# Opening of a two-layer trunk: modulation blocks that hold shifts and scales of the same 256 features, and a first double in pairs of contraction tiles

## The chip, the core and the metric

The kernel runs on one core of one Trainium2 chip. The metric is the device time of one execution in microseconds; the median of the runs counts. The core's engines run side by side and meet at semaphores: TensorE (PE, matrix products; its weight loads are PEld), VectorE (DVE), ScalarE (ACT), GpSimd (POOL) and SyncE (SP), which here issues DMAs.

## What is computed

Two trunk layers run over 128 context tokens and 512 denoising tokens, 1024 features wide. Each sub-layer is normed and modulated by vectors that come from a conditioning vector: c_ctx for the context tokens, c for the others. What matters here is the first sub-layer:

```
mod = (silu(c) @ w_mod[l] + b_mod[l]).reshape(1, 1, 3 * N_SUB, D_MODEL)
def modulated(j, y):
    return _rmsnorm(y, g[j]) * (1 + mod[:, :, 3 * j + 1]) + mod[:, :, 3 * j]
def _swiglu(h, w_in, w_out):
    g, u = jnp.split(h @ w_in, 2, axis=-1)
    return (jax.nn.silu(g) * u) @ w_out
x = x + 0.5 * mod[:, :, 2] * _swiglu(modulated(0, x), ffn_w_in[l, 0], ffn_w_out[l, 0])
```

So the first product of the network needs a shift (columns 0 to 1023 of w_mod[0]) and a scale (columns 1024 to 2047) for each of the 1024 features, each a sum over 1024 rows of w_mod.

## The kernel before

Tokens stand in the free dimension, features on the partitions: x is 8 tiles (kt = 0 to 7) of 128 features by 640 tokens. The tokens are handled in two halves of 320 (hf 0 and 1). A product in full precision is three matmuls (split_product): high part by high part, low by high and high by low, where the weights' parts are w_hi (ScalarE) and w_lo (VectorE) and the activations' parts b_hi and b_lo.

The two feed-forward products of a sub-layer are done in doubles of two output tiles of gate and of up. A double behind the first has seven items of 24 matmuls, which need sums and differences of the activations' quadrants (z11, z12, z21, z22; t1 and t2 are such sums; b_hi and b_lo hold seven forms of them). The first double of a sub-layer is plain: for a half hf, a tile k, a group g (gate or up) and a column block s there is one part (plain_part) of three matmuls: 64 parts, 192 matmuls. A part waits for the low part of its form and, at its group's first tile, for its w_lo (item_lo; one w_lo serves four tiles of one group).

Modulation for the first norm: the 2048 columns of w_mod are loaded as four blocks of 512 columns (mod_first), 2 MB each: 0 and 1 are shifts, 2 and 3 scales, and block 0 with block 2 serves tiles 0 to 3, block 1 with 3 tiles 4 to 7 (FIRST_ORDER). SyncE issues, in this order, the identity, x, seven small rows (b_mod, c_ctx, c, gains), block 0, block 2, the weights of the first two items, block 1, the weights of the other two, block 3. PE turns x into features (L1945), then the small rows (L1949), sums a block by 16 matmul instructions of 512 columns on four 32-row groups (mod_rows_of, L1970); ScalarE copies the sums out (keep_rows, L2583), PE multiplies them by pick, which turns them into columns on the partitions (turn_first, L1977), and VectorE adds the bias and multiplies (keep_first with keep_mod, L2698 and L2701). The inverse of the norm is spread over the partitions by PE (spread_first, L1959) and kept by ScalarE (L2068) in ss.

A tile then runs: VectorE scales x by ss (scale_form, L2754, two tiles at once), VectorE shifts the context tokens (L2763), ScalarE scales and shifts the rest (L2075) and makes b_hi (L2145, L2147, L2143), VectorE makes b_lo (L2829, L2824). The order on PE is written out in opening_double, on ScalarE and VectorE in opening_norm. Behind the forms VectorE makes t1 and t2 (L2848, L2850), products for the gate (L2846), sums of weights (L2664) and the w_lo of the second double (L2643). SyncE loads later blocks of w_mod (mod_grain, last_grain) once rows_free lets it; they are summed by features in instructions of 256 columns (mod_products, L1251) and turned by VectorE in squares of 32 (L2711).

## Time and profile before

| what | us |
|---|---|
| median of 3 runs | 2340.64 |
| the runs | 2340.48 to 2345.56 |
| profiled execution | 2343.96 |
| its span | 2342.2 |
| PE busy in the span | 2318.6 |
| first product of the first double | 29.27 |

The page gives busy time by engine, the chain of work that ended last, and groups of instructions by line. The chain is followed back from the end: each step goes to what released it. In the opening the timeline and the waits tell which engine is late; behind it the chain is almost one row of matmuls of line L1104. Matmul ends are modelled, so starts are what is read. A window gives the busy time of each engine in a stretch, the granted share of TensorE's clock and the DMA rate.

### The profile page before, as it was taken

Reading aid. Unit: us, or ns where it says so; the run is one execution under the profiler, and the core shown is the slowest. Engines: PE = TensorE matmul, PEld = TensorE weight load, DVE = VectorE, ACT = ScalarE, POOL = GpSimd, SP = SyncE. Lnnn points to the kernel's source line nnn. Section 1 sums busy time; section 2 is a strip of 40 time slices with the busy share of each in tenths; the row PEclk is TensorE's granted clock in tenths of the full one; section 3 lists DMA queues with packets and bytes.
Section 4 is the critical chain, followed back from the end, with each engine's and each line's share of the span. In section 5 each row is a group of like instructions: output and inputs, shape, how many; then the busy total and the mean of one; then the engine's idle time right before and its main releaser. Section 6 shows DMA issues by size and latency. Waiting matters only on the chain.

```text
span 2342.2 us, 39079 instructions
## 1 busy us (share of the span) xinstructions
PE 2318.6 (99%) x16276; PEld 2234.1 (95%) x16276; DVE 1567.4 (67%) x2376; ACT 955.7 (41%) x1501; POOL 30.5 (1%) x44
## 2 busy tenths in 40 slices
PE   7999999999999999999999999999999999999999
PEld 6999999988789999999999999999999999999999
DVE  4886776657867876777587777676245768467473
ACT  6532423443655523414364243244215355244242
POOL 0000000000001000000010000000000010000000
PEclk9999999999999999999999999999999999999999
DMA  8342554421101253334224344225221012322122
GB/s 299 126 145 90 198 162 139 150 89 54 57 19 55 91 162 127 122 112 148 88 92 160 114 156 148 87 77 173 87 75 46 19 55 73 108 73 91 57 97 73
DMA packets 199017, 251.56 MB, mean 107 GB/s; under 512 B 13026, under 2 KB 172602, under 8 KB 198842
## 3 DMA queue, kind: packets, MB, share of 16 engines
q1 hardware_dynamic: 198698, 249.00, 32.2%
q8 instruction: 129, 2.11, 0.4%
q14 instruction: 46, 0.38, 0.1%
q10 hardware_dynamic: 144, 0.07, 0.0%
HBM read 245.76 MB, written 3.28 MB: 106 GB/s over the span
## 4 chain that ended last, share of the span: by engine, by line
PE 94%; DVE 3%; ACT 2%; DMA 1%; issue 1%; SPq 0%; POOL 0%; DVEq 0%; ACTq 0%
PE banks L1104 82%; PE banks L1251 1%; PE banks L1428 1%; PE banks L1430 1%; PE banks L1429 1%; PE banks L1587 1%; DMA w_raw<-ffn_w_in 1%; PE banks L1575 1%; PE banks L1602 1%; PE banks L1796 0%; ACT w_hi L2032 0%; PE banks L1260 0%; PE banks L1970 0%; PE banks L1298 0%; DVE w_lo L2643 0%
## 5 line engine op out<-in xcount | busy, mean ns | idle before, releaser
L1104 PE MATMUL banks<-b_hi,w_hi 128*128 128x320 f32 x2496 | 776.9, 311 | 6.2 <-DVE b_lo L2829 3.5
L1104 PE MATMUL banks<-b_lo,w_hi 128*128 128x320 f32 x2496 | 772.2, 309 | 0.0
L1104 PE MATMUL banks<-b_hi,w_lo 128*128 128x320 f32 x2496 | 772.2, 309 | 0.0
L1104 PEld LDWEIGHTS banks<-b_hi,w_hi 128*128 128x128 f32 x2496 | 469.5, 188 | 20.2 <-issue 13.0
L2032 ACT ACTIVATE w_hi<-w_raw 128x1024 fp32r<-128x1024 f32 x296 | 310.2, 1056 | 401.9 <-PE banks L1104 226.1
L1104 PEld LDWEIGHTS banks<-b_lo,w_hi 128*128 128x128 f32 x2496 | 469.7, 188 | 0.0
L1104 PEld LDWEIGHTS banks<-b_hi,w_lo 128*128 128x128 f32 x2496 | 469.5, 188 | 0.0
L2643 DVE TENSOR_TENSOR w_lo<-w_raw,w_hi 128x1024 fp32r<-128x1024 f32 x296 | 361.5, 1223 | 150.2 <-ACT w_hi L2032 148.7
L1104 PE MATMUL banks<-hid_hi,w_hi 128*128 128x320 f32 x1664 | 400.2, 311 | 0.5 <-DVE hid_lo L2938 0.5
L1104 PE MATMUL banks<-hid_hi,w_lo 128*128 128x320 f32 x1664 | 396.2, 309 | 0.0
L1104 PE MATMUL banks<-hid_lo,w_hi 128*128 128x320 f32 x1664 | 396.1, 309 | 0.0
L1104 PEld LDWEIGHTS banks<-hid_hi,w_hi 128*128 128x128 f32 x1664 | 282.4, 188 | 2.1 <-issue 0.9
L1104 PEld LDWEIGHTS banks<-hid_lo,w_hi 128*128 128x128 f32 x1664 | 282.9, 188 | 0.0
L1104 PEld LDWEIGHTS banks<-hid_hi,w_lo 128*128 128x128 f32 x1664 | 282.4, 188 | 0.0
L2671 DVE SCALAR_TENSOR_TENSOR x<-banks,mod,x 128x128 f32<-128x128 f32 x354 | 135.1, 434 | 218.0 <-PE banks L1104 218.0
L2664 DVE TENSOR_TENSOR w_raw<-w_raw 128x1024 f32<-128x1024 f32 x160 | 195.4, 1222 | 17.6 <-DMA w_raw<-ffn_w_in 11.7
L2038 ACT ACTIVATE w_hi<-w_raw 128x1024 fp32r<-128x1024 f32 (+1 forms) x96 | 93.2, 984 | 233.4 <-PE banks L1104 233.2
L2217 ACT ACTIVATE hid_hi<-work 128x640 fp32r<-128x640 f32 x88 | 64.3, 735 | 155.3 <-DVE work L3023 142.0
L2649 DVE TENSOR_TENSOR w_lo<-w_raw,w_hi 128x1024 fp32r<-128x1024 f32 (+1 forms) x96 | 107.6, 1132 | 9.4 <-ACT w_hi L2038 8.7
L2990 DVE TENSOR_TENSOR work<-work,banks 128x320 f32<-128x320 f32 x80 | 38.1, 485 | 79.9 <-ACT work L2246 79.9
L2626 DVE TENSOR_TENSOR w_lo<-w_raw,w_hi 128x2048 fp32r<-128x2048 f32 (+1 forms) x24 | 52.8, 2201 | 54.7 <-ACT w_hi L2021 54.7
L2021 ACT ACTIVATE w_hi<-w_raw 128x2048 fp32r<-128x2048 f32 (+1 forms) x26 | 48.0, 1847 | 98.1 <-PE banks L1104 48.7
(339 smaller groups left out, 2409.1 us busy)
## 6 DMA issues: line engine op xcount, KB each, us to landing
w_raw<-ffn_w_in SPq DMA_DIRECT2D x176, 512.0 KB, 4.8
mod_grain<-w_mod SPq DMA_DIRECT2D x78, 512.0 KB, 5.9
w_raw<-ffn_w_out SPq DMA_DIRECT2D x64, 512.0 KB, 4.5
last_grain<-w_mod SPq DMA_DIRECT2D x40, 512.0 KB, 5.6
w_raw<-ffn_w_out SPq DMA_DIRECT2D x32, 384.0 KB, 3.7
w_raw<-w_in_odd SPq DMA_DIRECT2D x20, 512.0 KB, 4.7
mod_first<-w_mod SPq DMA_DIRECT2D x3, 2048.0 KB, 15.2
w_raw<-w_in_even SPq DMA_DIRECT2D x12, 512.0 KB, 4.9
```

What stands on the lines that cost most here:

```text
L1104: ins = pe.matmul(o, w3[w], v3[v][cols], start=first and i == 0, stop=last and i == 2, skip_group_check=onto_read)
L1251: ins = pe.matmul(bank[MODB][b * MOD_ROWS:(b + 1) * MOD_ROWS, 0:KIND_COLS], wide_c[:, kt, :], by_features(grain[q])[:, b], start=kt == 0, ...
L2021: act.activation(split_view(w_hi, kind, parity(unit)), raw_view(kind, parity(unit)), ACT.Copy).then_inc(hi_ready, 1)
L2032: act.activation(ring_in(w_hi, in_slot(d, t)), operand(d, t), ACT.Copy).then_inc(hi_ready, 1)
L2038: act.activation(ring_out(w_hi, out_slot(c, u), CHUNKS[c]), out_operand(c, u), ACT.Copy).then_inc(hi_ready, 1)
L2217: act.activation(hid_hi[:, k + s, :], work[:, s, 0:2, :].rearrange("p a b -> p (a b)"), ACT.Copy)\
L2626: dve.tensor_tensor(split_view(w_lo, kind, parity(unit)), raw_view(kind, parity(unit)), split_view(w_hi, kind, parity(unit)).bitcast(F32), ...
L2643: dve.tensor_tensor(ring_in(w_lo, q), operand(d, t), ring_in(w_hi, q).bitcast(F32), ALU.subtract).then_inc(lo_ready, 1)
L2649: dve.tensor_tensor(ring_out(w_lo, q, n), out_operand(c, u), ring_out(w_hi, q, n).bitcast(F32), ALU.subtract)\
L2664: dve.tensor_tensor(out_, in0, in1, op).then_inc(sums_done, 1)
L2671: ins = dve.scalar_tensor_tensor(out=xs, in0=bank[banks[hf]][:, in_bank], scalar=mod_col(v, layer, 3 * j + 2, d), in1=xs, op0=ALU.mult, op ...
L2990: dve.tensor_tensor(work[:, s, 1, :], work[:, s, 1, :], role(d, s, "C"), ALU.add).then_inc(c12_done, 1)
```

## The change

A block now holds 256 features' shifts and the same features' scales: block n serves the tiles 2n and 2n+1. It is loaded by two DMAs of 256 columns per row each (pieces of 1 KB in place of 2 KB); block 3 goes by four DMAs into the grain buffers and first_tail, after the sums of block 0. The order on SyncE is block 0, weights, block 1, block 2, weights, block 3. The seven small rows are issued by ScalarE.

The sums are taken by features: for each of 8 row tiles four instructions of 128 columns (64 on the engine, first_sums_of), and VectorE turns them in squares of 32 (first_turn). The copy by ScalarE, the turn by PE and pick are gone. SiLU comes ahead of the squares; of the ten copies of turned x ScalarE takes two (X_BY_ACT) and VectorE eight, before five and five.

The first double runs by pairs n of tiles: the four parts of half 0 for each tile of the pair, then the sums of block n+1, then three of four parts of half 1 (SUM_LESS leaves out group 1, block 1); the last part of each tile follows behind the last pair. The norm's work on ScalarE and VectorE follows in the same pairs, and the first sum of forms t1 stands behind pair 1.

```diff
         mod_first = [place(f"mod_first{r}", [P, KT, MOD_COLS], at=at) for r, at in
-                     enumerate((HB + TT * D * 4, HD_AT + 24576, HB + TT * D * 4 + block_bytes, HB + 71680 - block_bytes))]
+                     enumerate((HB + TT * D * 4, HD_AT + 24576, HB + 71680 - block_bytes))]
+        first_tail = place("first_tail", [P, 2, MOD_COLS], at=HB + TT * D * 4)
...
-        mod_rows = place("mod_rows", [P, 2, MOD_COLS], at=WORK + 5120)
+        first_turn = place("first_turn", [P, MOD_TILES, MOD_ROWS], at=WORK + 5120)
...
-        FIRST_BANK = (3, 2, 1, 7)
-        FIRST_SUM_BANK = (0, 1, 7, 7)
+        FIRST_SUM_BANK = (5, 1, 1, 1)
+        X_BY_ACT = (0, 2)
+        HEAD_LEAD = GRAIN_BUFS - 1
+        SUM_LESS = ((0, 0), (0, 1), (1, 0))
...
+        def first_rows(n, kt):
+
+            if n < QUAD - 1:
+                return mod_first[n][:, kt, :]
+            if kt < 2 * HEAD_LEAD:
+                return mod_grain[:, kt // 2, kt % 2 * MOD_COLS:(kt % 2 + 1) * MOD_COLS]
+            return first_tail[:, kt - 2 * HEAD_LEAD, :]
...
-            def load_first(r):
-                for hf in range(2) if r == 2 else (None,):
-                    ks = slice(0, KT) if hf is None else slice(HK * hf, HK * (hf + 1))
-                    sp.dma_start(mod_first[r][:, ks, :], w_mod[0][:, ks, r * MOD_COLS:(r + 1) * MOD_COLS])\
-                        .then_inc(mod_second_half_in if hf == 1 else mod_first_in[r], 16)
+            def load_first(n):
+
+                if n == QUAD - 1:
+                    sp.wait_ge(mod_first_sum, 1)
+                for j in range(2):
+                    c0 = j * D + n * (MOD_COLS // 2)
+                    src, cols = w_mod[0][:, :, c0:c0 + MOD_COLS // 2], slice(j * MOD_COLS // 2, (j + 1) * MOD_COLS // 2)
+                    if n < QUAD - 1:
+                        sp.dma_start(mod_first[n][:, :, cols], src).then_inc(mod_first_in[n], 16)
+                    else:
+                        lead = mod_grain[:, :, :].rearrange("p i (k c) -> p (i k) c", c=MOD_COLS)
+                        sp.dma_start(lead[:, :, cols], src[:, 0:2 * HEAD_LEAD, :]).then_inc(mod_first_in[n], 16)
+                        sp.dma_start(first_tail[:, :, cols], src[:, 2 * HEAD_LEAD:KT, :]).then_inc(mod_first_in[n], 16)
             load_first(0)
-            load_first(2)
             load_in(0, 0, 0)
             load_first(1)
+            load_first(2)
             load_in(0, 0, 1)
             load_first(3)
...
-            def opening_double(late_mod):
-
-                plain_parts(0, 0, range(2), range(2))
-                late_mod(0)
-                plain_parts(0, 0, range(2, HK), range(2))
-                late_mod(1)
-                plain_parts(0, 1, range(2), (0,))
-                late_mod(2)
-                plain_parts(0, 1, range(2, HK), (0,))
+            def opening_double(next_sums):
+
+                for n in range(QUAD):
+                    ks = range(2 * n, 2 * n + 2)
+                    plain_parts(0, 0, ks, range(2))
+                    if n == 0:
+                        pe.wait_ge(inverse_kept_in[1], 1)
+                    if n + 1 < QUAD:
+                        next_sums(n + 1)
+                        for k in ks:
+                            for g, s in SUM_LESS:
+                                plain_part(0, 1, k, g, s)
                 pe.wait_ge(first_kept, QUAD)
-                plain_parts(0, 1, range(HK), (1,))
-                plain_parts(0, 0, range(HK, KT), range(2))
-                plain_parts(0, 1, range(HK, KT), (0,))
-                plain_parts(0, 1, range(HK, KT), (1,))
+                for k in range(HK):
+                    plain_part(0, 1, k, 1, 1)
...
-            def mod_rows_of(r, into):
-
-                pe.wait_ge(mod_first_in[r], 16)
+            def first_sums_of(n):
+
+                sums = bank[FIRST_SUM_BANK[n]][:, 0:MOD_TILES * MOD_ROWS]
+                pe.wait_ge(mod_first_in[n], 16 * 2 if n < QUAD - 1 else 16 * 4)
+                if n > 0:
+                    pe.wait_ge(first_kept, n)
                 for kt in range(KT):
-                    if r == 2 and kt == HK:
-                        pe.wait_ge(mod_second_half_in, 16)
-                    group = slice(kt % 4 * MOD_ROWS, (kt % 4 + 1) * MOD_ROWS)
-                    ins = pe.matmul(into[group, :], wide_c[:, kt, :], mod_first[r][:, kt, :], start=kt < 4, stop=kt >= 4)
+                    cols = first_rows(n, kt).rearrange("p (m b c) -> p b m c", b=QUAD, c=MOD_ROWS)
+                    for b in range(QUAD):
+                        ins = pe.matmul(sums[b * MOD_ROWS:(b + 1) * MOD_ROWS, :], wide_c[:, kt, :], cols[:, b],
+                                        start=kt == 0, stop=kt == KT - 1)
                 ins.then_inc(mod_first_sum, 1)
 
-            def turn_first(n):
-
-                pe.wait_ge(mod_rows_ready, n + 1)
-                for m in range(MOD_TILES):
-                    ins = pe.matmul(bank[FIRST_BANK[n]][:, 2 * m:2 * m + 2], mod_rows[:, n % 2, m * P:(m + 1) * P], pick[:, :],
-                                    start=True, stop=True)
-                ins.then_inc(first_turned, 1)
-
+            spread_first(0)
             pe.wait_ge(silu_ready, 1)
-            pe.wait_ge(pick_ready, 1)
-            pe.wait_ge(x_kept_act, TT)
-            pe.wait_ge(x_kept_dve, TT)
-            mod_rows_of(0, bank[FIRST_SUM_BANK[0]])
-            for hf in range(2):
-                spread_first(hf)
-            turn_first(0)
-            mod_rows_of(2, bank[FIRST_SUM_BANK[1]])
-            turn_first(1)
-
-            def late_mod(step):
-
-                if step == 0:
-                    pe.wait_ge(inverse_kept_in[1], 1)
-                    mod_rows_of(1, bank[FIRST_SUM_BANK[2]])
-                elif step == 1:
-                    turn_first(2)
-                    mod_rows_of(3, bank[FIRST_SUM_BANK[3]])
-                else:
-                    turn_first(3)
-            ffn(0, late_mod, None, 1)
+            first_sums_of(0)
+            spread_first(1)
+            pe.wait_ge(x_kept_act, len(X_BY_ACT))
+            pe.wait_ge(x_kept_dve, 2 * TT - len(X_BY_ACT))
+            ffn(0, first_sums_of, None, 1)
...
-                    act.wait_ge(first_kept, 2 if kt < HK else QUAD)
+                    act.wait_ge(first_kept, kt // 2 + 1)
...
-            def opening_norm(keep_rows):
-
-                for kt in range(HK):
-                    if kt < 2:
-                        item_hi(0, 0, kt)
-                    form_high(0, 0, kt, 0)
-                for kt in range(HK):
-                    form_high(0, 0, kt, 1)
-                    if kt == 1:
-                        keep_rows(2)
-                item_hi(0, 0, 2)
-                item_hi(0, 0, 3)
-                keep_rows(3)
-                for hf in range(2):
-                    for kt in range(HK, KT):
-                        form_high(0, 0, kt, hf)
+            def opening_norm():
+
+                for n in range(QUAD):
+                    for hf in range(2):
+                        for kt in (2 * n, 2 * n + 1):
+                            if n == 0 and hf == 0:
+                                item_hi(0, 0, kt)
+                            form_high(0, 0, kt, hf)
+                    if n == 1:
+                        item_hi(0, 0, 2)
+                        item_hi(0, 0, 3)
                 sum_forms(0)
...
+            b_rows = a["b_mod"].rearrange("l (r p) -> l r p", p=P)
+            for l in range(DEPTH):
+                act.dma_start(small_rows[0:3 * N_SUB * KT, l, :], b_rows[l]).then_inc(rows_in, 16)
+            act.dma_start(small_rows[0:KT, 2, :], a["c_ctx"].rearrange("(r p) -> r p", p=P)).then_inc(rows_in, 16)
+            act.dma_start(small_rows[KT:2 * KT, 2, :], a["c"].rearrange("b (r p) -> (b r) p", p=P)).then_inc(rows_in, 16)
+            act.dma_start(small_rows[2 * KT:8 * KT, 2, :], a["norm_gain"].rearrange("l s (r p) -> (l s r) p", p=P))\
+                .then_inc(rows_in, 16)
+            act.dma_start(small_rows[64:68, 2, :], a["sgu_gain"].rearrange("e g p -> (e g) p")).then_inc(rows_in, 16)
+            act.dma_start(small_rows[68:72, 2, :], a["identity"][0:4, :]).then_inc(rows_in, 16)
+            act.wait_ge(rows_kept, 1)
+            given = rows_t[:, 0:2 * KT].rearrange("p (v k) -> p v k", v=2)
+            act.wait_ge(wide_cleared, 1)
+            act.activation(wide_c[:, :, 0:2].rearrange("p k v -> p v k"), given, ACT.Silu).then_inc(silu_ready, 1)
+            sqrt_table()
...
+                def scale_pair(n):
+                    for hf in range(2):
+                        scale_form(0, 0, slice(2 * n, 2 * n + 2), hf)
+
+                scale_form(0, 0, slice(0, 2), 0)
+                for n in range(QUAD):
+                    keep_first(n)
+                    for kt in (2 * n, 2 * n + 1):
+                        shift_first(kt)
+                        if n == 0:
+                            item_lo(0, 0, kt)
+                            if kt == 0:
+                                scale_form(0, 0, slice(0, 2), 1)
+                        low_form(0, slice(kt, kt + 1), 0)
+                    if n + 1 < QUAD:
+                        scale_pair(n + 1)
+                    low_form(0, slice(2 * n, 2 * n + 2), 1)
+                    if n == 1:
+                        first_form_sum(0)
+                        item_lo(0, 0, 2)
+                        item_lo(0, 0, 3)
...
             def keep_first(n):
 
-                r = FIRST_ORDER[n]
-                dve.wait_ge(first_turned, n + 1)
-                sums = bank[FIRST_BANK[n]][:, 0:2 * MOD_TILES].rearrange("p (m v) -> p v m", v=2)
-                keep_mod([sums[:, v, :] for v in range(2)], slice(MOD_TILES * r, MOD_TILES * (r + 1)))
+                def pair(tile):
+                    return tile[:, 0:2 * KT].rearrange("p (j k) -> p j k", j=2)[:, :, 2 * n:2 * n + 2]
+                dve.wait_ge(mod_first_sum, n + 1)
+                chain.inc(dve.transpose(first_turn[:, :, :].rearrange("p m c -> p (m c)"),
+                                        bank[FIRST_SUM_BANK[n]][:, 0:MOD_TILES * MOD_ROWS]))
+                chain.wait()
+                for v in range(2):
+                    chain.inc(dve.tensor_tensor(mod_tmp[:, v, :].rearrange("p (j k) -> p j k", j=2),
+                                                first_turn[:, :, v].rearrange("p (j k) -> p j k", j=2), pair(mod_add), ALU.add))
+                chain.wait()
+                for v in range(2):
+                    chain.inc(dve.tensor_tensor(pair(mod[:, v, :]), mod_tmp[:, v, :].rearrange("p (j k) -> p j k", j=2),
+                                                pair(mod_mul), ALU.mult))
+                chain.wait()
                 dve.sem_inc(first_kept, 1)
```

Two places in the order of the built programs. On PE, from the end of the turns of x to the second half's first products: before, two blocks' sums and two turns stand ahead of the first product.

```order
L1949 MATMUL banks_5<-ident,small_rows 128x72 x3
L1970 MATMUL banks_1<-mod_first_93,wide_c 32x512 x8
L1959 MATMUL banks_7<-ident,x_rms 128x128 x2
L1959 MATMUL banks_7<-ident,x_rms 128x64 x2
L1959 MATMUL banks_7<-ident,x_rms 128x128 x2
L1977 MATMUL banks_3<-pick,mod_rows 128x2 x4
L1970 MATMUL banks_1<-mod_first_95,wide_c 32x512 x8
L1977 MATMUL banks_3<-pick,mod_rows 128x2 x4
L1104 MATMUL banks_3<-b_hi,w_hi 128x320
L1104 MATMUL banks_3<-b_lo,w_hi 128x320
L1104 MATMUL banks_3<-b_hi,w_lo 128x320
```

After (order of the changed kernel): one block's sums stand there, between the two spreads.

```order
L1961 MATMUL banks_1<-ident,x_rows 128x128 x8
L1971 MATMUL banks_7<-ident,x_rms 128x128 x2
L1971 MATMUL banks_7<-ident,x_rms 128x64
L1984 MATMUL banks_5<-mod_first_92,wide_c 32x128 x32
L1971 MATMUL banks_7<-ident,x_rms 128x64
L1971 MATMUL banks_7<-ident,x_rms 128x128 x2
L1108 MATMUL banks_3<-b_hi,w_hi 128x320
L1108 MATMUL banks_3<-b_lo,w_hi 128x320
L1108 MATMUL banks_3<-b_hi,w_lo 128x320
```

What moved: the small rows' turn to the front, the second block's sums behind 24 products, and the steps with pick away.

On VectorE, from the last work on tile 3 to the first low part of tile 4: before, one w_lo, then columns, scalings, another w_lo, columns.

```order
L2824 TENSOR_TENSOR b_lo<-z_81,b_hi 128x640 x2
L2643 TENSOR_TENSOR w_lo<-w_raw,w_hi 128x1024
L2698 TENSOR_TENSOR mod_tmp<-banks_1,mod_add 128x4 x2
L2701 TENSOR_TENSOR mod<-mod_tmp,mod_mul 128x4 x2
L2754 TENSOR_TENSOR z_83<-x,ss 128x640 x2
L2643 TENSOR_TENSOR w_lo<-w_raw,w_hi 128x1024
L2698 TENSOR_TENSOR mod_tmp<-banks_7,mod_add 128x4 x2
L2701 TENSOR_TENSOR mod<-mod_tmp,mod_mul 128x4 x2
L2763 TENSOR_SCALAR z_a<-z_a,mod 128x128 x4
L2829 TENSOR_TENSOR b_lo<-z_a,b_hi 128x320 x2
```

After, between the low part of the wide half of tiles 2 and 3 and the first low part of tile 4:

```order
L2802 TENSOR_TENSOR b_lo<-z_80,b_hi 128x640
L2818 TENSOR_TENSOR t_83<-z_80,z_a 128x1280
L2632 TENSOR_TENSOR w_lo<-w_raw,w_hi 128x1024 x2
L3587 STREAM_TRANSPOSE first_turn<-banks_1 128x128
L3591 TENSOR_TENSOR mod_tmp<-first_turn,mod_add 128x4 x2
L3595 TENSOR_TENSOR mod<-mod_tmp,mod_mul 128x2x2 x2
L2741 TENSOR_SCALAR z_a<-z_a,mod 128x128
L2807 TENSOR_TENSOR b_lo<-z_a,b_hi 128x320
```

What moved: t_83 (before it was t_84, behind all forms) and both w_lo stand in a row ahead of the columns of block 2.

## Rows read from the trace of the kernel before

**Rows 1.** The page: busy time of TensorE, and the chain that ended last.
```profile
PE 2318.6 (99%) x16276; PEld 2234.1 (95%) x16276; DVE 1567.4 (67%) x2376; ACT 955.7 (41%) x1501; POOL 30.5 (1%) x44
...
PE 94%; DVE 3%; ACT 2%; DMA 1%; issue 1%; SPq 0%; POOL 0%; DVEq 0%; ACTq 0%
```

**Rows 2.** The chain in order of time, 60 to 120 us: start, us, what.
```profile
59.86 23.61 PE banks L1104 x161
83.48 1.86 PE banks L1251 x32
```

**Rows 3.** The same chain, 0 to 60 us.
```profile
11.02 1.14 ACT squares L2571 x2
...
16.80 2.87 PE banks L1970 x16
...
29.27 6.21 PE banks L1104 x24
35.47 1.85 PE banks L1970 x16
37.32 3.71 PE banks L1104 x24
41.04 0.79 PE banks L1977 x8
...
43.68 1.95 PE banks L1104 x12
...
46.42 13.59 PE banks L1104 x92
```

**Rows 4.** Waits of PE, 0 to 120 us: in total, times, longest.
```profile
PE banks L1104 <- DVE b_lo L2829: 3.0, 1, 3.0
```

**Rows 5.** DMA issues up to 60 us: count, KB each, us to landing.
```profile
x_rows<-x_prompt SPq DMA_DIRECT2D x1, 512.0 KB, 3.9
...
ident<-identity SPq DMA_DIRECT2D x1, 64.0 KB, 2.0
```

**Rows 6.** Windows: stretch, length, busy us (instructions) per engine, PEclk, DMA share, GB/s.
```profile
0.00:9.60 9.60, 3.87 (x17) 3.50 (x18) 1.65 (x9) 3.70 (x6) 0.20 (x4) 1.00 0.79 290
...
17.70:21.00 3.30, 3.30 (x19) 1.61 (x11) 0.19 (x1) 1.24 (x3) 0.00 (x0) 0.50 1.05 383
21.50:23.50 2.00, 2.00 (x23) 1.39 (x25) 0.54 (x5) 0.55 (x2) 0.00 (x0) 1.00 1.10 348
...
28.00:34.60 6.60, 5.33 (x20) 5.37 (x21) 6.56 (x13) 5.68 (x11) 0.00 (x0) 0.50 1.07 369
```

**Rows 7.** Timeline, VectorE and ScalarE, 24 to 29 us: start, duration, operation.
```profile
24.90 0.82 DVE L2754 TENSOR_TENSOR z<-x,ss 128x640 f32<-128x640 f32 x1
26.33 0.23 DVE L2698 TENSOR_TENSOR mod_tmp<-banks,mod_add 128x4 f32<-128x4 f32 x2 [0.61 <-PE banks L1977]
...
27.24 1.22 DVE L2643 TENSOR_TENSOR w_lo<-w_raw,w_hi 128x1024 fp32r<-128x1024 f32 x1
...
28.63 0.48 DVE L2829 TENSOR_TENSOR b_lo<-z_a,b_hi 128x320 fp32r<-128x320 f32 x1
...
25.08 1.05 ACT L2032 ACTIVATE w_hi<-w_raw 128x1024 fp32r<-128x1024 f32 x1
26.92 0.55 ACT L2075 ACTIVATE z_a<-z_a,mod 128x192 f32<-128x192 f32 x1 [0.79 <-DVEq L3609]
27.50 0.47 ACT L2145 ACTIVATE b_hi<-z_a 128x320 fp32r<-128x320 f32 x1
```

**Rows 8.** The tile mod_turn: min/median/max ns of the transposition.
```profile
L2711 DVE STREAM_TRANSPOSE mod_turn<-banks x32: 307/314/318, 128.6 to 1642.1; 128x128 f32<-128x128 f32 x32
```

**Rows 9.** Timeline of VectorE, 55 to 76 us.
```profile
55.23 0.83 DVE L2829 TENSOR_TENSOR b_lo<-z,b_hi 128x640 fp32r<-128x640 f32 x1 [1.28 <-ACT b_hi L2143]
55.97 1.48 DVE L2848 TENSOR_TENSOR t<-z,z_a 128x1280 f32<-128x1280 f32 x1
...
74.58 1.22 DVE L2643 TENSOR_TENSOR w_lo<-w_raw,w_hi 128x1024 fp32r<-128x1024 f32 x1
```

125 lines of the change are left out of this document (36 added, 89 removed).

## The prediction

> **What bounds the kernel now.** I read the page's busy shares and its chain first [rows 1]: TensorE (PE) is busy 99% of a span of 2342.2 us and carries 94% of the chain that ended last. So a microsecond counts only if it moves the row of matmuls on PE. The chain behind the opening is that row alone: 161 products in 23.61 us, 0.1466 us each, then modulation sums, then products again [rows 2]. Nothing there depends on the clock on the wall, so what the opening gains at its last wait is kept to the end; what it gains before that can be lost again. The chain of the opening [rows 3] shows where PE starts its first product: 29.27, after a wait of 3.0 us for the first low part [rows 4]. From there PE never waits before 120 us (the other waits of that list lie ahead of 29.27). The first double has 192 products; before, they end at 46.42 + 132 x 0.1466 = 65.8.
>
> **The start.** Everything here is re-laid, so I walk the new order with the old durations. SyncE no longer issues the seven small rows; ScalarE does, at 0.3 to 0.4 us each, the last at about 3. No row shows such a DMA land in the shadow of the x rows. The identity alone took 2.0 us, the x_prompt rows 3.9 [rows 5]; I take 4.0 for each, the side of the one that shared the stream, so the last is in at 6.9. PE turns them first, VectorE copies, SiLU ends at 8.6, a table load of 1.3 at 9.9, two x copies at 0.5 and five squares at 1.14 [rows 3] end at 17.1, the root, its reciprocal and PE's spread of the first half at 18.2.
> In sentences that the rest can do without: the Trainium skill, page "DMA: Bandwidth & Descriptors", section "Issuing engines are not separate DMA queues", says that DMAs of different issuing engines share the same 16 DMA engines and interleave, so that a second issuer saves issue time alone. No row of before has two issuers at once. By it the rows still compete with x, which speaks against the early end of my bounds, not for a later start than the rival below.
> Block 0 lands in time: 2.8 MB were through by 9.6 at 290 GB/s [rows 6], and the blocks, now in pieces of 1 KB, should go at the 348 GB/s of the stretch of 1 KB weights (21.5 to 23.5) and not at the 383 of the blocks of before (17.7 to 21.0) [rows 6]. That is 2.1 MB, 15.6, plus about 1 us until the semaphore, 16.8; the first weights (1 MB) then land at 19.8. Block 3 lands near 41, far ahead of its use at 49, so the slower pieces cost nothing; w_raw too is covered.
> Sums of block 0: now 64 instructions of 128 columns instead of 16 of 512. Before, 16 of 512 took 1.85 [rows 3] and 32 of 256 took 1.86 [rows 2]: the same columns, the same time, whatever the cut. I take 1.86 for 64 of 128 too. The other end is that an instruction doesn't get shorter than the 0.058 of the 256-column ones: 3.7 per block.
> So: 18.2 + 1.9 = 20.1, spread of the second half 20.7, ScalarE keeps it 21.2, w_hi 1.05, w_lo 1.22, one scaling 0.82 (pitch 0.75), b_lo 0.48 [rows 7]. The column work (transposition 0.31 [rows 8], two additions and two products 0.23 a pair [rows 7]) lies beside the ScalarE steps. PE starts at **24.6**, 4.65 earlier than 29.27.
>
> **The rest of the first double.** I take the first 24 products as before, 6.2, most of them at half clock: granted 0.50 in 28.0 to 34.6, the lower of the two levels of 1.2 and 2.4 GHz, after PE had stood idle before 29.27 [rows 6]. A run of products behind other work costs 0.19 more than its count (24 in 3.71, 12 in 1.95 [rows 3]). The new order on PE: 24 products to 30.8; sums of block 1, 32.7; 18 products, 35.5; 24 products, 39.0; sums of block 2, 40.9; 18 products, 43.7. Now the pair 4, 5 must be ready, and it isn't. VectorE has done the pair 2, 3 at 36.7, then stand two scalings (1.5), a low part of 0.82 that waits for ScalarE until 38.4, the first sum of forms (1.48) and two w_lo (2.3): it is free at 42.8, 1.6 after the sums came. Then transposition, columns, shift, b_hi and b_lo (0.9 + 0.55 + 0.47 + 0.48, with handing over): 45.3. **A new stall of 1.6 us.** Go on: 24 products to 48.8; sums of block 3, 50.7; 18 products, 53.5 (they cover the same chain of 2.6 for the last pair); 66 products, 63.2. Against 65.8 that is 2.6 earlier. The sum of it: start +4.65, two turn steps of 0.79 gone behind the start [rows 3], one more block's sums on the path -1.86, one switch more -0.2, stall -1.6.
>
> **The work behind it, where VectorE was nearly late already.** In before VectorE runs without a gap from its last wide b_lo at 55.23 to the w_lo at 74.58, which ends at 75.80 [rows 9]. PE reads that weight in item 3 of the second double, which starts two items of 24 products ahead of 83.48 [rows 2]: 76.44. The slack was 0.6. After: sums of block 3 seen by VectorE at 51.1, columns 52.0, four shifts with their b_hi on ScalarE (0.95 to 1.05 each with handing over, [rows 7]) and one wait for a shift to 56.5, b_lo at 56.6. From 55.23 to 75.80 are 20.57; the first sum of forms (1.48, pitch 1.52 [rows 9]) was done earlier, which leaves 19.05: 75.65. PE arrives at 63.2 + 3 x 3.52 = 73.8. **PE waits 1.9 us**, and item 3 starts at 75.7 instead of 76.44. Of 4.65 us at the start 0.7 are left. Behind that the order on all engines is the old one.
>
> **The sum.** The profiled execution takes 2343.96 (span 2342.2), the median of the runs is 2340.64, 3.3 below, with runs to 2345.56; the saving is taken off the median: 2340.64 - 0.7 = 2339.9. A difference under 0.3% (7 us) is about what a measurement of this kernel can't tell from no change.
>
> **The rivals.**
> 1. The wait at item 3 isn't there, because VectorE or ScalarE runs its stretch some tenths quicker at each handing over, or the rows land early (2.0 each, the low bound, is 0.8 more). For it: the wait is the difference of two long walks. Against: VectorE had no idle time there to give. Then all 2.6 are kept: 2338.0, and with the higher clock a few products sooner 2337.
> 2. The half clock or late rows take the start: slower than before. PE stands idle from about 14 to 17.6, as it did ahead of 16.80, where the clock went to 0.50 in 17.7 to 21.0 [rows 6] and the sums took 2.87 instead of 1.85 [rows 3]. With sums and spreads of block 0 wholly at half clock the start moves by up to 2.5, with rows landing only behind all of x (9.6) by 3.4. It decides from a start 0.7 later than 24.6, since from there on all goes through ScalarE's and VectorE's chain to item 3. Part of the delay comes back when the higher clock comes at an earlier product; net 0.9 to 2.2 slower than before: 2341.5 to 2342.8. For it: the same idle time, the same place. Against: the spread and the sums begin sooner after the last turn.
> 3. Sums by 128 columns cost as much an instruction as those of 256. Then 1.86 more in each of four blocks, 7.4, less the stall of 1.6 which they cover, and some 0.8 less because the higher clock comes at an earlier product: 5.0 against my walk: 2344.9. Against it: the time followed the columns and not the count from 16 to 32 instructions. The Trainium skill, page "TensorE: Matmul & The Clock Gate", section "Wait — 56ns, not 53.3ns?", knows a floor of about 62 ns a matmul when the sequencer's microcode decodes it, which would be 4.0 a block and about 2346 by the same sum; the 0.058 of the 256-column row is already below that, so the trace speaks against it.
> 4. That the change doesn't do what it says: a pair can't start as its block lands, since block 1 and 2 land (23 and 29) long before PE asks for them (31 and 39). That is so in my own walk: PE and VectorE set the pace, not the blocks. It has no time of its own.
>
> **Chances.** My forecast (2338.7 to 2341.3, its own range) 0.5; rival 1 0.2; rival 2 0.22; rival 3 0.05; something else 0.03. I predict **2339.9**. The range goes down to 2337.0 (rival 1 with the clock) and up to 2343.5 (rival 2 whole, and a median that falls on one of the long runs as before had one). Faster by over 0.3% needs 7 us, more than the whole gain at the start: 0.02. Slower by as much needs rival 3 and more: 0.03. Within: 0.95.
>
> **What the profile after would show.** First product near 24.6; two new waits in PE's list, one for b_lo of about 1.6 near 44 and one for w_lo of about 1.9 near 74; the four sums at 1.9 each; the modulation sums that stood at 83.48 at about 82.8. Wrong would be the walk of the start if the first product comes before 23.5 or after 27, the stall terms if PE waits for neither, and the price of the sums if a block takes over 2.3 at full clock.

## The result

The changed kernel takes 2347.64 us (median of 15 runs, 2346.04 to 2351.74); the kernel before, run beside it, 2342.08 (15 runs, 2340.47 to 2345.56). The ratio is 1.0023, with a 95% interval of 1.0016 to 1.0030: slower, by less than the 0.3% that I took for the least that can be measured; the interval leaves out 1. The forecast was 2339.9, its range ended at 2343.5. It was wrong.

The profiled execution took 2346.87, its span is 2345.1. The page of after; busy time of TensorE, and the shares of the chain that ended last:

```profile
PE 2316.1 (99%) x16436; PEld 2236.8 (95%) x16436; DVE 1570.5 (67%) x2383; ACT 950.6 (41%) x1494; POOL 30.5 (1%) x44
...
PE 90%; DVE 5%; ACT 2%; issue 1%; DMA 1%; ACTq 0%; SPq 0%; DVEq 0%; POOL 0%
```

The chain's share on VectorE went from 3% [rows 1] to 5%. The opening is only a part of that: added up from the chain's pieces, VectorE's work in it grew from 2.6 to 19.2 us between 0 and 120 us, and from none to 33 us between 700 and 1000 us, a stretch in which TensorE's waits add up to 0.2 us in after and to none in before. So the share alone says little about what was lost. The chain of after in order of time (start, us, what) up to the first product:

```profile
3.24 5.40 DMA small_rows<-identity
...
8.78 0.61 PE banks L1949 x3
...
9.67 0.23 ACT wide_c L2562
9.92 1.28 ACT L2049
...
17.04 1.16 ACT squares L2573 x2
...
18.80 1.29 PE banks L1971 x6
20.08 3.08 PE banks L1984 x64
23.16 0.88 PE banks L1971 x6
...
27.99 5.90 PE banks L1108 x24
```

The small rows land 5.4 us after their issue, all else on ScalarE stands behind them, the sums of block 0 take 3.08, and the first product comes at 27.99: 1.3 earlier than before (29.27 in [rows 3]), not 4.65. The same chain behind it:

```profile
33.89 1.93 PE banks L1984 x64
...
42.64 1.40 DVE t L2818
44.04 2.27 DVE w_lo L2632 x2
```

```profile
48.89 5.29 PE banks L1108 x24
54.18 1.88 PE banks L1984 x64
56.07 12.61 PE banks L1108 x84
...
79.60 1.15 DVE w_lo L2632
80.79 7.30 PE banks L1108 x48
88.09 1.86 PE banks L1261 x32
```

The last row is my mark for all that follows: **the modulation sums**, the first work of TensorE that both kernels do in the same place. It stood at 83.48 [rows 2] and stands at 88.09, 4.6 later. The opening has lost 4.6 us, though its first product is 1.3 earlier. The waits of TensorE up to 120 us (in total, times, longest):

```profile
PE banks L1108 <- DVE b_lo L2807: 5.9, 2, 4.0
PE banks L1971 <- DVE x_rms L3580: 3.3, 1, 3.3
PE banks L1108 <- DVE w_lo L2632: 1.5, 1, 1.5
```

One wait for b_lo is the start (4.0), the other, 1.9, is the new one between 46.8 and 48.9, and the wait for w_lo is the one ahead of 80.79. Both were foretold. What was not stands in the windows (stretch, length, busy us of PE, PEld, DVE, ACT, POOL, granted clock, DMA share, GB/s):

```profile
20.00:23.10 3.10, 3.10 (x66) 2.72 (x65) 0.82 (x1) 0.44 (x1) 0.00 (x0) 0.59 1.10 349
...
28.00:32.70 4.70, 4.70 (x18) 4.70 (x19) 3.84 (x6) 2.50 (x5) 0.00 (x0) 0.50 1.10 348
...
46.70:48.80 2.10, 0.22 (x2) 0.00 (x0) 1.24 (x7) 1.45 (x3) 0.00 (x0) 1.00 0.63 171
49.80:53.20 3.40, 3.40 (x15) 3.40 (x14) 2.59 (x4) 1.80 (x4) 0.00 (x0) 0.50 0.35 123
```

The granted clock is 0.50 (the lower of 1.2 and 2.4 GHz) three times: in the sums of block 0 (0.50 from 20.1 to 22.0; the window above, 0.59, goes on to where it rises), in the first products, and once more behind the gap at pair 4, 5, where 15 matmuls take the time of 24. In before the row was at full clock from 34.7 on. So 24 products take 5.29 there instead of 3.5.

### The profile page after: what moved, and what is told of

It is laid out like the page before. It is cut to its first block, busy times and chain, and to the rows that moved or that the text cites. A ratio compares the mean times of both kernels' runs of the same rounds, so it can differ in the third digit from the quotient of the medians.

```text
span 2345.1 us, 39402 instructions
## 1 busy us (share of the span) xinstructions
PE 2316.1 (99%) x16436; PEld 2236.8 (95%) x16436; DVE 1570.5 (67%) x2383; ACT 950.6 (41%) x1494; POOL 30.5 (1%) x44
## 4 chain that ended last, share of the span: by engine, by line
PE 90%; DVE 5%; ACT 2%; issue 1%; DMA 1%; ACTq 0%; SPq 0%; DVEq 0%; POOL 0%
PE banks L1108 78%; PE banks L1261 1%; DMA w_raw<-ffn_w_in 1%; PE banks L1439 1%; PE banks L1440 1%; PE banks L1438 1%; DVE w_lo L2632 1%; PE banks L1597 1%; PE banks L1585 1%; PE banks L1612 1%; DVE w_raw L2653 1%; ACT w_hi L2024 1%; PE banks L1806 0%; PE banks L1270 0%; PE banks L1308 0%
```

## The theories

**Theory 1.** The opening is slower because of four things that can be told apart: the start is late (small rows, clock); VectorE's queue makes TensorE stand at pair 4, 5; that standing lowers the clock, which costs about as much again; and VectorE's chain from the sums of block 3 to the fourth weight of the second double makes it stand once more. **Rivals:** the clock falls at its own times, whatever TensorE does; VectorE and ScalarE set the pace, so that a quicker TensorE only waits longer; the small rows' place doesn't matter. Each run is read at its modulation sums, against 88.09 (and 83.48); eight of the eleven have a single execution, so their times are not compared.

## The middle gap

**The first sum of forms later.**

```diff
                     if n == 1:
-                        first_form_sum(0)
                         item_lo(0, 0, 2)
                         item_lo(0, 0, 3)
+                    if n == 2:
+                        first_form_sum(0)
```

> The changed kernel with one edit: VectorE makes the first sum of forms (z12 - z11, 1.49 us) behind the column work and low parts of pair 4, 5 instead of ahead of the column work, in the stretch 52.6 to 56.1 where it was idle. Theory 1 (VectorE's queue makes TensorE's gap at 46.61 to 48.89, and this gap lets the granted clock fall to 0.50 in 49.83 to 53.24, which costs another 1.8): the gap shrinks from 2.28 to 0.8, the clock stays at 1.0, the 24 products behind it take 3.5 instead of 5.3, and the modulation sums that stand at 88.09 stand near 84.9 (3.2 earlier). Rival (the clock falls at that time whatever TensorE does there): gap 0.8, but the 24 products still at 5.3, sums near 86.6. Rival (the gap is the two low weights or ScalarE's): the gap stays over 2, sums near 88.

The chain of this run:

```profile
47.64 3.76 PE banks L1108 x24
...
78.00 7.30 PE banks L1108 x48
85.30 1.86 PE banks L1261 x32
```

The gap fell from 2.28 to 0.86 (start to start, 46.78 to 47.64), the 24 products took 3.76, and the sums came at 85.30: 2.8 earlier (3.2 expected). One instruction of VectorE of 1.4 us cost twice that. The wait for the fourth weight stayed (76.17 to 78.00).

**The gap filled.** This tells the clock from the gap: the gap stays, but TensorE isn't idle in it.

```diff
                     ks = range(2 * n, 2 * n + 2)
+                    if n == 2:
+                        pe.wait_ge(first_kept, 3)
+                        for _ in range(12):
+                            pe.transpose(bank[1][:, 512 - P:512], ident[:, :], ident[:, :])
                     plain_parts(0, 0, ks, range(2))
```

> The changed kernel with one addition: in the gap ahead of pair 4, 5 TensorE waits for the column work of block 2 (done near 47.1) and then turns the identity 12 times into a bank that is free, 1.3 us, which nothing waits for. The gap as the products see it stays (2.1 between the end of one and the start of the next), VectorE's order stays. Clock theory (TensorE standing idle lets the clock fall, 1.8 us for the 24 products behind): no fall in 49.8 to 53.2, the 24 products in 3.5 instead of 5.2, the modulation sums of 88.09 near 86.3, nothing else changed. Rival (the fall belongs to the late pair itself, VectorE and ScalarE being slow to hand over, not to the clock): the 24 products still at 5.2, sums at 88.

Window and chain:

```profile
49.30:52.70 3.40, 3.40 (x24) 3.40 (x24) 2.59 (x5) 2.51 (x5) 0.00 (x0) 1.00 0.64 217
```

```profile
49.24 3.75 PE banks L1108 x24
...
86.90 1.86 PE banks L1265 x32
```

The gap is as long as it was (46.97 to 49.24), the clock stays at 1.00, and 24 matmuls fit where 15 did. The small rows came later in this execution (9.5), so the first product stood at 28.64; from there to the sums it is 58.26 against 60.10 in after. 0.3 of that lies in the first products; behind the gap it is 5.29 against 3.75. **The clock behind the gap costs 1.5 us by itself**, and it falls because TensorE stood idle. With the 1.4 of the gap that makes 2.9; the run before gained 2.8, since its first 24 products took 0.15 longer than in after.

## The start

**The idle times of the start filled.**

```diff
+            for t in range(1, TT + 1):
+                pe.wait_ge(sums_ready, t)
+                fill(7)
             spread_first(0)
...
             pe.wait_ge(x_kept_dve, 2 * TT - len(X_BY_ACT))
+            fill(30)
```

(fill(n) turns the identity n times into bank 4, which has no other use then.)

> The changed kernel with TensorE kept at work in its two idle times of the start, by turns of the identity into a bank that is free then: 7 behind each of the five squares (about 0.8 us each at full clock), and 30 (3.3 us) behind the spread of the second half. Nothing waits for them. Theory 1 (idle time of TensorE lets the clock fall, and the lower clock takes 1.2 us of the sums of block 0 and 2.2 us of the first 24 products): clock 1.0 from 12 on, sums of block 0 in 1.9 instead of 3.1, first product near 26.8 instead of 27.99, 24 products in 3.7 instead of 5.9, and the gap at pair 4, 5 and the wait for the third weight of the second double are passed on as they are, so the modulation sums of 88.09 stand near 84.6. Rival (VectorE and ScalarE set the pace of the first double, so products that are quicker only wait longer): the start's 1.2 is kept, but the gap at pair 4, 5 grows by up to 2.2, sums near 86.8. Rival (the fall is not of TensorE's idle time): first product at 28.0 and sums at 88.

```profile
19.95 1.88 PE banks L1988 x64
...
30.86 1.93 PE banks L1988 x64
...
45.85 5.29 PE banks L1108 x24
...
85.05 1.86 PE banks L1261 x32
```

The sums take 1.88, the first product is at 26.66, the next sums at 30.86 (33.89 in after), and the modulation sums 3.04 earlier. All that the start and the first 24 products give arrives there: the gap at pair 4, 5 (43.59 to 45.85) and the wait for the fourth weight are as long as before. The rival, a gap that grows, falls.

**The rows issued by SyncE again.** The seven issues stand behind x on SyncE as in before; the order on TensorE and ScalarE is that of after.

```diff
-                act.dma_start(small_rows[0:3 * N_SUB * KT, l, :], b_rows[l]).then_inc(rows_in, 16)
+                sp.dma_start(small_rows[0:3 * N_SUB * KT, l, :], b_rows[l]).then_inc(rows_in, 16)
...
```

> The changed kernel with the seven small rows issued by SyncE behind x and ahead of block 0, as in the kernel before, and not by ScalarE; TensorE still turns them first. It prices what ScalarE's issue bought. Rows theory (the DMAs of both issuers share the same engines, and the rows land when x is through, 8.8 by ScalarE, 10.6 for the last of x): by SyncE they land at 11 to 12, the spread comes 2.5 to 3 later than 18.80, block 0 and the weights 2.9 us of issue later, first product near 30.5, sums of 88.09 near 90.6. Rival (where they are issued doesn't matter): landing under 9.8, first product at 28. Rival (the clock decides: rows later give less idle time ahead of the sums of block 0, which then run at full clock): spread later by 2.5 but first product only 1.3 later.

```profile
5.07 6.51 DMA small_rows<-identity
...
22.62 1.88 PE banks L1993 x64
...
89.09 1.86 PE banks L1270 x32
```

The rows land 2.9 later (TensorE starts on them at 11.72), the spread 2.9 later (21.74), but the first product only 1.3 (29.33), and the modulation sums only 1.0: the clock did not fall ahead of the sums of block 0, and they took 1.88 and not 3.08. The third expectation was the right one. ScalarE's issue buys 2.9 us of landing, of which 1.3 reach the first product.

Is it the shorter idle time of TensorE ahead of the spread (2.9, not 3.3) that kept the clock up? The runs that do not fill it fit this at this place: behind 3.3 us (after, first sum later, first weight early, gap filled) and 4.1 (behind what has landed) the sums ran at half clock, behind 2.9 (here) and 2.8 (fourth weight) at full clock. But behind the idle time of 2.0 at pair 4, 5 the clock fell in every run that had it, this one too. So the length alone doesn't decide it, and what does stays open. In the run of the fourth weight the kernel is that of after up to there, and its chain shows that the fall differs from one execution to the next:

```profile
19.96 0.88 PE banks L1971 x6
20.84 1.88 PE banks L1984 x64
```

**Behind what has landed.** TensorE turns four groups of x ahead of the small rows, ScalarE makes two squares ahead of SiLU.

```diff
             for t in range(TT):
                 n = 2 * t
+                if t == 2:
+                    act.wait_ge(rows_kept, 1)
+                    act.wait_ge(wide_cleared, 1)
+                    act.activation(wide_c[:, :, 0:2].rearrange("p k v -> p v k"), given, ACT.Silu).then_inc(silu_ready, 1)
+                    sqrt_table()
...
```

> The changed kernel with the small rows moved back behind what has landed before them: TensorE turns x of the prompt and of the first block of samples (four groups) ahead of the small rows, VectorE copies two of these groups first, and ScalarE makes the first two squares and x copies ahead of SiLU. Theory 1 (the small rows landed at 8.78, and all five squares stood behind them, which set the spread at 18.80): the last square ends near 15.0 instead of 18.2, the spread is at 15.6, and the sums of block 0 begin when the block is in (16.7) at half clock, 3.1 long, so the first product comes near 24.9 instead of 27.99 and all behind it 3 earlier, the modulation sums of 88.09 near 85.1. Rival (the clock in the first products counts more than their start): the first product near 24.9, but its lower clock lasts as many us as before, so the sums stand between 85 and 86.5. Rival (ScalarE's handing over to VectorE, not the squares, sets the start): first product not before 27.

The timeline of ScalarE:

```profile
10.58 1.28 ACT L2566 ACT_TABLE_LOAD   x1
11.87 0.23 ACT L2566 ACTIVATE wide_c<-rows_t 128x16 f32<-128x16 f32 x1
12.12 1.28 ACT L2050 ACT_TABLE_LOAD   x1
```

A miss: the spread came at 17.74, not 15.6, the modulation sums at 87.30, not 85.1. Of the 2.1 us, 1.28 are a table load that I had left out: SiLU behind copies and squares needs one of its own, beside that for the root; in after the first load was hidden at 3.69, when ScalarE had nothing to do. And the earlier sums ran at half clock again (3.55).

**The first weight's high part early.**

```diff
-            for hf in range(2):
-                keep_inverse_of(0, hf)
+            keep_inverse_of(0, 0)
+            item_hi(0, 0, 0)
+            keep_inverse_of(0, 1)
...
                 scale_form(0, 0, slice(0, 2), 0)
+                item_lo(0, 0, 0)
                 for n in range(QUAD):
...
```

> The changed kernel with one edit at the start: ScalarE makes the high part of the first weight (1.05) between the two halves of the kept inverse and not behind both, and VectorE its low part (1.22) ahead of the column work of block 0. The weight has landed at 18.14, so both steps find idle time (ScalarE stood idle for 3.5 ahead of 24.06). Theory 1 (the first product waits for a chain in which these two steps stand behind the sums of block 0): the first product comes near 25.8 instead of 27.99, and all behind it moves with it as long as VectorE keeps up, the modulation sums of 88.09 stand near 85.9. Rival (the first product is earlier, but its half-clock time of 6.8 us begins when TensorE begins, or the idle time ahead is too short to lower the clock): first product near 25.8, the 24 products anywhere between 3.7 and 6.2, sums between 83.8 and 86.2. Rival (another chain sets the start): not before 27.

```profile
26.19 5.46 PE banks L1108 x24
...
85.84 1.86 PE banks L1261 x32
```

Nearly as expected (25.8): the first product 1.8 earlier, the modulation sums 2.25 earlier: the first 24 products took 5.46 and not 5.90, since the clock was back at 1.00 from 30 on and not from 32.7. The 18.14 of the expectation is only the first of the weight's two pieces. ScalarE waits for both, and the second landed at 19.65 in after and at 19.54 here, still ahead of the step at 20.07.

## The fourth weight of the second double

```diff
+                if f == 0:
+                    item_lo(f, 1, 3)
                 dve.wait_ge(sums_of_forms_ready, 4 * f + 2)
                 dve.tensor_tensor(z21, z21, t2[:, :, :], ALU.subtract).then_inc(sums_of_forms_ready, 1)
-                item_lo(f, 1, 3)
+                if f > 0:
+                    item_lo(f, 1, 3)
```

> The changed kernel with one edit in the first work of the second double: VectorE makes the low part of the fourth weight (1.22) ahead of the last form (z21 - t2, 1.48) and not behind it. TensorE waits 1.84 for that weight at 78.95 to 80.79. Theory 1 (VectorE's chain from the sums of block 3 to this weight sets the wait): the wait falls by 1.4 to 0.4, the modulation sums of 88.09 stand near 86.7, and no other wait takes its place. Rival (ScalarE's high part of that weight or of the last form comes next): the wait falls by under 0.5, or another of 1 or more appears in the next item, sums at 88. In the first double nothing changes: first product 28.0, gap 2.3 at 46.6.

The waits of TensorE, and its chain:

```profile
PE banks L1108 <- ACT work L2226: 1.2, 1, 1.2
```

```profile
79.93 7.27 PE banks L1108 x48
87.20 1.86 PE banks L1261 x32
```

The rival holds: the weight is ready 1.1 ahead of the product, but now TensorE waits 1.2 for the banks that ScalarE empties (L2226), behind the same weight's high part. Of 1.5 us of wait 0.3 went. In after ScalarE emptied these banks at 80.3, only 0.4 ahead of VectorE's weight, so moving one step of one of the two buys almost nothing.

## The kernel before, with its idle times filled

> The kernel before with TensorE kept at work in its two idle times of the start: 30 turns of the identity into a free bank behind the turn of the small rows (12.7 to 16.0), 24 behind the turn of the second block (26.3 to 28.9). Clock theory: 1.0 from 11 on, sums of the first block in 1.9 instead of 2.9, first product near 28.4 instead of 29.27, 24 products in 3.7 instead of 6.2. What then reaches the end is the question. Theory 1 (VectorE's chain had 0.6 of slack at the fourth weight of the second double, so TensorE's gain is lost there unless VectorE's chain starts earlier too): a wait for w_lo of 1 to 2 us appears near 74, and the modulation sums that stand at 83.48 stand near 81.7, so 1.8 of the 3.4 is kept. Rival (TensorE's row alone counts): no wait, sums at 80.1. Rival (the clock isn't held by such turns): 83.5. The time: 1.8 less than the kernel before by theory 1, hardly to be told from the same.

The edit: fill(30) behind the turn of the small rows, fill(24) behind that of the second block. Windows and chain:

```profile
16.50:18.40 1.90, 1.90 (x17) 0.51 (x17) 0.19 (x1) 1.53 (x2) 0.00 (x0) 1.00 1.05 387
```

```profile
24.00 15.12 DMA mod_first<-w_mod
...
39.16 1.92 PE banks L1974 x16
...
80.88 1.86 PE banks L1251 x32
```

The sums come at 80.88, 2.6 ahead of before, and the time is 2340.24 (10 runs, 2339.09 to 2342.22) against 2343.70 of the kernel before beside it (19 runs): ratio 0.9987, interval 0.9978 to 0.9996. My theory had expected a wait for w_lo of 1 to 2 us; there is none. The error was to call 0.6 us a slack in time. VectorE's chain starts at the sums of the last block, which moved too: that weight was ready at 73.2 here, and TensorE used it at 73.8. What counts is the work that TensorE has between those sums and the weight. Of the 3.4 us that the rival had expected 2.6 came; block 3 landed at 39.12, and TensorE waited 0.4 for it.

## Three, five and six edits together

Three: fill in the start (18 turns ahead of the first product, not 30), first sum of forms later, first weight early.

> The changed kernel with three edits together: TensorE kept at work in its idle times of the start (7 turns behind each square, 18 ahead of the first product), the first sum of forms behind pair 4, 5, and the first weight split early. Theory 1 (the start's two edits add up, and with no lower clock the products run at 3.7 for 24): first product near 24.7, gap at pair 4, 5 at most 1 and no fall of the clock behind it, the modulation sums of 88.09 near 79.9 (2.2 + 3.1 + 2.8 earlier). It is late if the weights for pair 4, 5 or block 3 (landed at 35.6 and 41.6) come too late now: then a wait on a DMA ahead of 45 and sums near 81. Against the kernel before (83.48) 3.5 earlier.

The modulation sums came at 81.11, 7.0 earlier than in after; 79.9 had been expected. The missing 1.2 is a first product at 25.37 (24.7 expected) and a stop of 0.6 us six products later, for the second weight.

Five: also the small rows behind x, weight_sum(0, 1, 0) ahead of the last wide low part, and the fourth weight ahead of the last form.

> The three edits, and two more: the small rows behind x of the prompt and the first samples (the spread came 1.1 earlier with it), and VectorE's first work of the second double re-laid: the first weight sum (1.22) ahead of the last wide low part, where VectorE was idle for 1.7, and the fourth weight's low part ahead of the last form. Theory 1 (the wait for w_lo of 1.8 is VectorE's and ScalarE's chain from the sums of block 3, and falls with each step taken out of it): first product near 23.8, the wait for the fourth weight under 0.6, the modulation sums of 88.09 near 77.8, 5.7 ahead of the kernel before, and its time some 5 to 6 below it (ratio 0.9977). Rival (landing of block 3 and its weights now sets the pace): waits on DMAs near 36 to 42, sums near 80, time 3 to 4 below before.

```profile
72.74 7.28 PE banks L1108 x48
80.02 1.86 PE banks L1261 x32
```

8.1 earlier than after, 3.5 ahead of before; 2.2 short of what I expected. The wait ahead of 72.74 is still 1.2, most of it again for ScalarE's banks. The time is 2339.46 (10 runs, 2337.69 to 2342.11), ratio 0.9985, interval 0.9976 to 0.9995.

Six, against the run with five: the high parts of both first weights ahead of the kept inverse; VectorE's first low part also goes ahead of its first scaling, and 17 turns replace 18.

```diff
+            item_hi(0, 0, 0)
             keep_inverse_of(0, 0)
-            item_hi(0, 0, 0)
+            item_hi(0, 0, 1)
             keep_inverse_of(0, 1)
...
```

> The five edits together with a sixth: both first weights' high parts go ahead of the halves of the kept inverse on ScalarE, and VectorE's first low part ahead of its first scaling. In the run with five, the first product stood at 24.82 and six products later TensorE waited 0.78 for the second weight. Theory 1 (VectorE's low part at 21.02 to 22.16 pushed the column work of block 0 back by 0.9, and the second weight's high part stood behind two steps): first product near 24.0, no wait after the sixth product, the modulation sums of 79.95 near 78.4, the time 1.5 below the run with five and some 6 below the kernel before (ratio 0.998 to 0.9975). Rival (the weights for pair 4, 5, landed at 35.6, or block 3 come next): a wait near 36 to 42, sums near 79.5.

The timeline of ScalarE:

```profile
20.30 1.06 ACT L2033 ACTIVATE w_hi<-w_raw 128x1024 fp32r<-128x1024 f32 x1 [1.89 <-DMA w_raw<-ffn_w_in]
```

Wrong: the weight landed at 20.28, the high part waited 1.9 for it and held up the kept inverse behind it. First product 25.93, modulation sums 80.83; time 2339.64 (11 runs), ratio 0.9985, interval 0.9976 to 0.9994. The weights' landing is now what the start waits for. Both of these kernels beat before by as much as the old kernel with its idle times filled does (ratios 0.9985, 0.9985 and 0.9987, with intervals that overlap almost wholly); the three can't be told apart. None of them ran beside after, whose own ratio to before is 1.0023. So no run shows a gain of the re-laid order over the old one.

## Why the prediction was wrong, step by step

| step, us | forecast | measured in after | difference |
|---|---|---|---|
| first product | 24.6 | 27.99 | +3.4 |
| its 24 products | 6.2 | 5.9 | -0.3 |
| sums and products to pair 4, 5 | 12.9 | 12.9 | 0 |
| stall there | 1.6 | 2.1 | +0.5 |
| 24 products behind it | 3.5 | 5.3 | +1.8 |
| to the fourth weight | 25.0 | 24.9 | -0.1 |
| wait for it | 1.9 | 1.7 | -0.2 |
| 48 products to the modulation sums | 7.1 | 7.3 | +0.2 |
| modulation sums | 82.8 | 88.09 | +5.3 |

**The start: wrong, and by the sign I had set (over 27).** Of its 3.4 us, 1.1 are the small rows, a term that was sized too small: I took 4.0 for each behind its issue, "the side of the one that shared the stream"; it was 5.4 (8.64 instead of 6.9; 0.6 was caught up by shorter hand-overs), and 5.4 to 6.6 in the other executions. The last piece is 2 KB; the identity, 64 KB and first in the stream, took 2.0. So it isn't the size of the piece that sets the time; that it is the rest of the stream fits, but no run took x away. The Trainium skill, page "DMA: Bandwidth & Descriptors", section "Issuing engines are not separate DMA queues", says that DMAs interleave on the same 16 DMA engines whichever engine issued them, and that a second issuer saves the time of issuing alone. The runs fit it: by SyncE the last issue came 1.8 later (5.07, not 3.24) and the landing 2.9 later, and the other 1.1 is within what the time to landing differs by from one execution to the next. 0.8 are root, reciprocal and spread of the first half: I gave them 1.1 together, they took 1.9 (0.31, 0.20 and 1.29). 1.2 are the sums of block 0 at half clock, and 0.3 the spread of the second half and the chain behind it.

**The clock: the step that failed.** The walk put the sums of block 0 at 1.9 and the 24 products behind the stall at 3.5, both at full clock; they took 3.08 and 5.29, at half clock. Rival 2 had the mechanism of the start, the idle time ahead of the sums and a clock of 0.50 in them, and I gave it 0.22 although I could name "the same idle time, the same place". What I set against it, "the spread and the sums begin sooner after the last turn", was weak: TensorE was idle for 3.3 us ahead of the spread (3.72 in before). It deserved more than 0.22, though it was not certain: in two runs with 2.8 and 2.9 us idle there the clock stayed up. (Its 3.4 for rows that land behind all of x doesn't follow from its 9.6, which is 2.7 behind 6.9.) The spread belongs to the same loss: where the clock stayed up it took 0.88 and not 1.29, so of the 0.8 above 0.4 is the clock too, and with the 1.2 of the sums it took 1.6 us ahead of the first product. And rival 2 stopped at the start. I forecast a gap of 1.6 in the middle of the row and kept full speed behind it, where the rows of before showed that a gap of 3.0 [rows 4] was followed by half clock [rows 6]. Filling the gap shows that this alone is 1.5 us (the other 0.3 of the table is that a run of products behind a stop begins slower than my 3.52). With both in the sum the walk would have given 82.8 + 1.6 + 1.5 = 85.9, and 2343.1 from the same median: slower than before, near the upper end of my range.

**The middle stall: right.** Pair 4, 5 was late by VectorE's queue, in the order that I had written down. It was 0.5 longer: from the end of the sums of block 1 to the first product of the pair I walked 12.6, it took 13.1. 0.3 of that lies ahead of the wide low part of pair 2, 3 (41.81), on a way on which VectorE stood idle three times for ScalarE's b_hi, 0.60 to 0.68 each; 0.1 lies in the three steps behind it, and 0.1 in the columns, shift and low part of the pair.

**The tail: right.** The wait for the fourth weight was 1.7 against 1.9. The runs show what it is made of better than my text did. TensorE has 156 products, 23.0 us, between the sums of block 3 and that weight; VectorE needs 24.7. The difference was the same (1.81 to 1.84 from the start of one product to the start of the next) in every run in which the order behind these sums was left alone, whether their end stood at 49.09 (three edits) or at 57.08 (rows by SyncE). So whatever is won ahead of them arrives in full, and "of 4.65 us at the start 0.7 are left" was the price of this fixed difference. Before had 32.8 us of TensorE's work there: the change put the last block's sums behind 60 more products.

**Prices that held.** 64 instructions of 128 columns took 1.88 to 1.93 at full clock: the time follows the columns, rival 3 falls. The blocks in pieces of 1 KB came at 346 to 352 GB/s and landed at 16.65, 25.66, 32.63 and 41.58, ahead of their sums at 20.08, 33.89, 42.1 and 54.18: hidden, as said.

**From the opening to the median.** 2347.64 is 7.7 above the forecast: 5.3 are the steps above, 1.4 that the kernel before itself has a median of 2342.08 with fifteen runs and not the 2340.64 of three, and 1.0 is left. It can't be given a place: behind the modulation sums one execution takes 2258.7 (before), 2257.0 (after), and between 2256.9 and 2261.3 in the others, in steps that differ from one execution to the next. Much of it is waits of TensorE for VectorE's work (L2979 in after) of up to 1.6 us, most behind 800 us, in the old kernel with its idle times filled also at 220: behind 200 us they add up to 1.6 in after and to 4.6 in the run that took 2261.3. I didn't follow why they differ. Why the medians differ by 5.6 and the openings by 4.6 stays open.

## What to carry to other kernels

An idle time of TensorE is to be priced twice: its length, and the half clock in the work behind it. Here idle times of 2.0 to 4.0 us mostly cost 1.2 to 2.2 more each, and that cost vanished when work that nobody needs was put into them, in the old kernel as in the new; two of 2.8 and 2.9 us cost nothing more, so that such a term is a likely one and not a certain one. When a chain of another engine starts at an event that the change moves, compare durations from that event (TensorE's work against VectorE's) instead of dates; and when one step is moved off such a chain, look at the engine that ends right behind it.

## What was not expected of the hardware

- A gap of 2.3 us from the start of one matmul to that of the next (46.61 to 48.89) was followed by 3.4 us at half clock, one of 0.9 (46.78 to 47.64) was not. Idle times of 2.8 and 2.9 ahead of the spread were not followed by it either.
- The same small rows, issued by ScalarE at the same time, were turned at 8.78, 9.48 and 9.94 in different executions of kernels that are alike up to there; the one with the latest rows had the clock at 1.00 in the sums of block 0 and the earliest first product (27.55, against 27.99 and 28.64).
- Four matmuls of 128 columns on the four 32-column groups start 6 to 7 ns apart, and the next four 109 ns behind the first of them, so 64 of them cost what 16 of 512 columns do.
- SiLU behind copies and squares needed a table load of its own, 1.28, though ScalarE had loaded a table at 3.55. Whether squares run from the table of SiLU isn't shown: the load for the root stood ahead of the next squares.
